# The passages between stages of a two-layer trunk without GpSimd: squares summed on TensorE tile by tile, residual adds and sums on VectorE

## The reference

```python
def rms_norm(x, g, eps=NORM_EPS):
    xf = x.astype(jnp.float32)
    y = xf * lax.rsqrt(jnp.mean(xf * xf, axis=-1, keepdims=True) + eps)
    return (y * g.astype(jnp.float32)).astype(x.dtype)

def sq_relu_mlp(x, w_in, w_out):
    return jnp.square(jax.nn.relu(x @ w_in)) @ w_out

    h = x
    for layer in range(DEPTH):
        hn = rms_norm(h, norm_mix_pre[layer])
        ...  # m = mixer_ab(hn, ...) in layer 0, mixer_ret(hn, ...) in layer 1
        h = h + rms_norm(m, norm_mix_post[layer])
        f = sq_relu_mlp(rms_norm(h, norm_ffn_pre[layer]), ffn_w_in[layer], ffn_w_out[layer])
        h = h + rms_norm(f, norm_ffn_post[layer])
    return h
```

## Time and profile before

| | |
|---|---|
| Median of three runs | 1648.21 us |
| The profiled execution's own time | 1650.05 us |
| Its span, first to last instruction | 1648.2 us |
| Mean granted TensorE clock, as a share of full speed | 0.962 |
| TensorE matmuls busy | 1542.7 us (94%) |
| VectorE busy | 817.7 us (50%) |
| ScalarE busy | 479.5 us (29%) |
| GpSimd busy | 76.0 us (5%) |

### The profile page before, as it was taken

The page is one execution under the profiler, slowest core; times in us unless marked ns, Lnnn a source line. Parts: engine busy times, 40 slices in busy tenths (PEclk is TensorE's granted clock), DMA queues, the critical chain, the costliest instruction groups (busy, mean ns, idle before and its releaser), DMA issues.

```text
span 1648.2 us, 23178 instructions
## 1 busy us (share of the span) xinstructions
PE 1542.7 (94%) x10440; PEld 1247.2 (76%) x10440; DVE 817.7 (50%) x1003; ACT 479.5 (29%) x521; POOL 76.0 (5%) x73
## 2 busy tenths in 40 slices
PE   6898999987689999999899999998997999999996
PEld 5676867766578888888787787877876888888885
DVE  5637547274475444535463444434335754444444
ACT  4325143332332222212332223122123422212220
POOL 1000000000020000000120000000001200000001
PEclk9899998989789999999899999999998999999998
DMA  4111011010032222222221221212211222222221
GB/s 167 52 41 57 15 52 45 28 52 3 26 115 102 101 82 99 102 102 94 72 91 51 78 102 51 102 52 77 102 52 51 94 85 102 103 102 85 94 102 51
DMA packets 19298, 125.16 MB, mean 76 GB/s; under 512 B 2240, under 2 KB 2240, under 8 KB 5120
## 3 DMA queue, kind: packets, MB, share of 16 engines
q1 hardware_dynamic: 18800, 121.29, 21.1%
q0 software_dynamic: 400, 2.39, 0.4%
HBM read 121.58 MB, written 2.10 MB: 75 GB/s over the span
## 4 chain that ended last, share of the span: by engine, by line
PE 87%; DVE 5%; ACT 3%; DMA 2%; issue 2%; POOL 0%; POOLq 0%; SPq 0%; DVEq 0%; ACTq 0%
PE bank L292 23%; PE bank L298 22%; PE bank L295 22%; PE bank L555 7%; PE bank L1119 2%; PE bank L1096 2%; PE bank L1090 2%; PE bank L1093 2%; DMA raw<-weights 1%; PE bank L306 1%; DVE WL L265 1%; PE bank L1111 1%; ACT WH L259 1%; PE bank L569 1%; PE bank L312 1%
## 5 line engine op out<-in xcount | busy, mean ns | idle before, releaser
L292 PE MATMUL bank<-XH,WH 128*128 128x512 f32 x944 | 386.4, 409 | 31.4 <-DVE WL L265 16.2
L295 PE MATMUL bank<-XL,WH 128*128 128x512 f32 x944 | 373.5, 396 | 0.0
L298 PE MATMUL bank<-XH,WL 128*128 128x512 f32 x944 | 373.5, 396 | 0.0
L265 DVE TENSOR_TENSOR WL<-raw,WH 128x2048 fp32r<-128x2048 f32 (+1 forms) x113 | 254.5, 2253 | 203.6 <-ACT WH L259 203.6
L259 ACT ACTIVATE WH<-raw 128x2048 fp32r<-128x2048 f32 (+1 forms) x113 | 212.2, 1878 | 379.0 <-DMA raw<-weights 379.0
L292 PEld LDWEIGHTS bank<-XH,WH 128*128 128x128 f32 x944 | 180.7, 191 | 74.0 <-issue 33.0
L298 PEld LDWEIGHTS bank<-XH,WL 128*128 128x128 f32 x944 | 180.7, 191 | 39.4
L295 PEld LDWEIGHTS bank<-XL,WH 128*128 128x128 f32 x944 | 181.2, 192 | 35.1 <-issue 0.7
L292 PE MATMUL bank<-AH,WH 128*128 128x512 f32 x512 | 199.4, 389 | 0.0
L298 PE MATMUL bank<-AH,WL 128*128 128x512 f32 x512 | 199.2, 389 | 0.0
L295 PE MATMUL bank<-AL,WH 128*128 128x512 f32 x512 | 199.2, 389 | 0.0
(11 more groups left out here) (256 smaller groups left out, 1727.3 us busy)
## 6 DMA issues: line engine op xcount, KB each, us to landing
raw<-weights SPq DMA_DIRECT2D x109, 1024.0 KB, 4.8
h<-x_fm SPq DMA_DIRECT2D x4, 512.0 KB, 6.9
raw<-weights SPq DMA_DIRECT2D x4, 512.0 KB, 3.7
out_fm<-h SPq DMA_DIRECT2D x8, 256.0 KB, 2.0
rc<-ret_const POOLq DMA_DIRECT2D x1, 1536.0 KB, 6.8
stage<-pairs POOLq DMA_DIRECT2D x4, 199.0 KB, 2.7
cst<-const SPq DMA_DIRECT2D x1, 641.0 KB, 10.1
vec<-vectors SPq DMA_DIRECT2D x1, 41.5 KB, 1.7
```

The lines of the kernel that those rows point to most:

```text
L265: nc.vector.tensor_tensor(WL[i][:, :n], raw[i][:, :n], WH[i][:, :n], ALU.subtract).then_inc(S("w_lo"), 1)
L292: mm = pe.matmul(bank[b][:], wh, xh, start=(k == 0), stop=False)
L295: mm = pe.matmul(bank[b][:], wh, xl, start=False, stop=False)
L298: mm = pe.matmul(bank[b][:], wl, xh, start=False, stop=(k == len(xs) - 1))
```

## The change

GpSimd no longer takes part in any norm or residual. Four things change:

1. The squares of f go to TensorE one tile at a time (`post_tile_pe`), eight calls of `token_sums` into bank 4 in place of three. In the feed-forward blocks tile t is taken behind output unit t + 1 of the last quarter, so tiles 0 to 6 stand in the loop and tile 7 behind it. After the mixers and after retention tile t is taken behind unit t + 2, and tiles 6 and 7 behind the loop. `post_sum_pool` and `post_sum_dve` are gone.
2. The squares of h: VectorE adds squares 0 to 5 in five adds (`pre_sum_dve`), interleaved with the residual's tiles from the fourth on; TensorE takes this sum and squares 6 and 7, three calls in place of two. `pre_sums_pool` is gone.
3. All eight adds to h are VectorE's, each behind the XL of the tile before.
4. GpSimd waits for the end of the first residual, issues the DMA of the retention constants, and then does its adds inside the retention stage, as before.

```diff
@@ -313,22 +313,24 @@
             return mm
 
         def pre_sums_pe(pe, m):
-            pe.wait_ge(S("hsq_sum_a"), 3 * m + 3)
+            pe.wait_ge(S("hsq_sum"), 5 * m + 5)
             token_sums(pe, 4, sum_a, True, False)
-            pe.wait_ge(S("hsq_sum_b"), 3 * m + 3)
-            token_sums(pe, 4, sum_b, False, True).then_inc(S("pre_sums"), 1)
+            for kt in (6, 7):
+                pe.wait_ge(S("hsq"), m * KT + kt + 1)
+                mm = token_sums(pe, 4, sq[:, kt, :], False, kt == 7)
+            mm.then_inc(S("pre_sums"), 1)
 
         def pre_spread_pe(pe, m):
             pe.wait_ge(S("pre_rstd"), m + 1)
             spread(pe, 5, pre_rstd).then_inc(S("pre_spread"), 1)
 
-        def post_norm_pe(pe, m):
-            pe.wait_ge(S("fsq_sum_a"), 3 * m + 3)
-            token_sums(pe, 4, sum_a, True, False)
-            pe.wait_ge(S("fsq_sum_b"), 2 * m + 2)
-            token_sums(pe, 4, sum_b, False, False)
-            pe.wait_ge(S("fsq"), m * KT + KT)
-            token_sums(pe, 4, sq[:, KT - 1, :], False, True).then_inc(S("post_sums"), 1)
+        def post_tile_pe(pe, m, kt):
+            pe.wait_ge(S("fsq"), m * KT + kt + 1)
+            mm = token_sums(pe, 4, sq[:, kt, :], kt == 0, kt == KT - 1)
+            if kt == KT - 1:
+                mm.then_inc(S("post_sums"), 1)
+
+        def post_spread_pe(pe, m):
             pe.wait_ge(S("post_rstd"), m + 1)
             spread(pe, 5, post_rstd).then_inc(S("post_spread"), 1)
 
@@ -374,44 +376,19 @@
             nc.vector.scalar_tensor_tensor(XL[:, kt, :], h[:, kt, :], gain(layer, kind, kt), XH[:, kt, :],
                                            ALU.mult, ALU.subtract).then_inc(S("x_lo"), 1)
 
-        def pre_sums_dve(dve, m):
-            for i in range(3):
-                dve.wait_ge(S("hsq"), m * KT + 2 * i + 3)
-                if i:
-                    dve.wait_ge(S("hsq_sum_a"), 3 * m + i)
-                nc.vector.tensor_tensor(sum_a, sum_a if i else sq[:, 0, :], sq[:, 2 * i + 2, :],
-                                        ALU.add).then_inc(S("hsq_sum_a"), 1)
-
-        def pre_sums_pool(pool, m):
-            for i in range(3):
-                pool.wait_ge(S("hsq"), m * KT + 2 * i + 4)
-                if i:
-                    pool.wait_ge(S("hsq_sum_b"), 3 * m + i)
-                nc.gpsimd.tensor_tensor(sum_b, sum_b if i else sq[:, 1, :], sq[:, 2 * i + 3, :],
-                                        ALU.add).then_inc(S("hsq_sum_b"), 1)
+        def pre_sum_dve(dve, m, i):
+            dve.wait_ge(S("hsq"), m * KT + i + 2)
+            if i:
+                dve.wait_ge(S("hsq_sum"), 5 * m + i)
+            nc.vector.tensor_tensor(sum_a, sum_a if i else sq[:, 0, :], sq[:, i + 1, :], ALU.add).then_inc(S("hsq_sum"), 1)
 
         def pre_rstd_dve(dve, m):
             dve.wait_ge(S("pre_root"), m + 1)
             nc.vector.reciprocal(pre_rstd, pre_root).then_inc(S("pre_rstd"), 1)
 
-        def post_sum_pool(pool, m):
-            for i in range(3):
-                pool.wait_ge(S("fsq"), m * KT + 2 * i + 3)
-                if i:
-                    pool.wait_ge(S("fsq_sum_a"), 3 * m + i)
-                nc.gpsimd.tensor_tensor(sum_a, sum_a if i else sq[:, 0, :], sq[:, 2 * i + 2, :],
-                                        ALU.add).then_inc(S("fsq_sum_a"), 1)
-
-        def post_sum_dve(dve, m, i):
-            dve.wait_ge(S("fsq"), m * KT + 2 * i + 4)
-            if i:
-                dve.wait_ge(S("fsq_sum_b"), 2 * m + i)
-            nc.vector.tensor_tensor(sum_b, sum_b if i else sq[:, 1, :], sq[:, 2 * i + 3, :],
-                                    ALU.add).then_inc(S("fsq_sum_b"), 1)
-
-        def add_to_h(ops, kt):
-            ops.tensor_tensor(h[:, kt, :], h[:, kt, :], hn[:, kt % 2, :],
-                              ALU.add).then_inc(S("h_odd" if kt % 2 else "h_even"), 1)
+        def add_to_h(kt):
+            nc.vector.tensor_tensor(h[:, kt, :], h[:, kt, :], hn[:, kt % 2, :],
+                                    ALU.add).then_inc(S("h_odd" if kt % 2 else "h_even"), 1)
 
 
 
@@ -425,16 +402,13 @@
                         h_is_ready(dve, m, kt - 2)
                     nc.vector.scalar_tensor_tensor(hn[:, kt % 2, :], f[:, kt, :], gain(*post, kt),
                                                    bank[5][:], ALU.mult, ALU.mult).then_inc(S("post_term"), 1)
-                    if kt % 2 == 0:
-                        dve.wait_ge(S("post_term"), m * KT + kt + 1)
-                        add_to_h(nc.vector, kt)
                 if kt and pre:
                     x_low(dve, m + 1, *pre, kt - 1)
-
-        def residual_pool(pool, m):
-            for kt in range(1, KT, 2):
-                pool.wait_ge(S("post_term"), m * KT + kt + 1)
-                add_to_h(nc.gpsimd, kt)
+                if kt < KT:
+                    dve.wait_ge(S("post_term"), m * KT + kt + 1)
+                    add_to_h(kt)
+                if pre and kt >= 3 and kt < KT:
+                    pre_sum_dve(dve, m + 1, kt - 3)
 
         def add_to_f(dve, use, b, m, first):
             n = use.next(b)
@@ -472,7 +446,10 @@
                         left = 0 if k else 2 if q == 0 and j == 4 else 1
                         units(pe, use, [(j + k) % 4], [columns(cj, k)], X if j < 8 else A, left,
                               a_tile if j == 8 and k == 0 else None)
-            post_norm_pe(pe, m)
+                        if q == QUARTERS - 1 and j + k > 8:
+                            post_tile_pe(pe, m, j + k - 9)
+            post_tile_pe(pe, m, KT - 1)
+            post_spread_pe(pe, m)
 
         def ffn_act(act, use, c0, m, layer):
             for q in range(QUARTERS):
@@ -512,8 +489,6 @@
                                                 ALU.subtract).then_inc(S("a_lo"), 1)
                     else:
                         add_to_f(dve, use, b, j - 8, q == 0)
-                        if q == QUARTERS - 1 and j in (12, 14):
-                            post_sum_dve(dve, m, j // 2 - 6)
                     if j % 2 == 0 and (q or j):
                         split_lo(dve, c0 + 8 * q + j // 2 + 2)
 
@@ -1027,7 +1002,11 @@
         def last_out_pe(pe, use):
             for m in range(KT):
                 out_unit(pe, use, m, PAIRS - 1)
-            post_norm_pe(pe, 0)
+                if m >= 2:
+                    post_tile_pe(pe, 0, m - 2)
+            for kt in range(KT - 2, KT):
+                post_tile_pe(pe, 0, kt)
+            post_spread_pe(pe, 0)
 
         def last_out_act(act, use):
             for m in range(KT):
@@ -1039,8 +1018,6 @@
         def last_out_dve(dve, use):
             for m in range(KT):
                 add_to_f(dve, use, out_bank(m, PAIRS - 1), m, False)
-                if m in (4, 6):
-                    post_sum_dve(dve, 0, m // 2 - 2)
                 if m == 5:
                     split_lo(dve, FFN0_CHUNK + 1)
 
@@ -1142,7 +1119,11 @@
                     else:
                         for i in range(2):
                             units(pe, use, [RET_OUT[j + i]], [ws[i]], B, 1 if j == 4 and i == 0 else 0)
-            post_norm_pe(pe, m)
+                            if hd == RET_HEADS - 1:
+                                post_tile_pe(pe, m, j + i - 2)
+            for kt in range(KT - 2, KT):
+                post_tile_pe(pe, m, kt)
+            post_spread_pe(pe, m)
 
         def ret_act(act, use, m):
             for hd in range(RET_HEADS):
@@ -1265,8 +1246,6 @@
                     add_to_f(dve, use, RET_OUT[j], j, hd == 0)
                     if j % 4 == 1:
                         split_lo(dve, c + 8 + j // 4)
-                    if hd == RET_HEADS - 1 and j in (4, 6):
-                        post_sum_dve(dve, m, j // 2 - 2)
 
         def ab_uses(use):
             for j in range(2):
@@ -1317,22 +1296,14 @@
                 nc.gpsimd.tensor_copy(pp[:, Q_LNW:], stage[:, Q_LNW:]).then_inc(S("norm_vectors"), 1)
                 pool.wait_ge(S("pp_ready"), p + 1)
                 pool.wait_ge(S("norm_vectors"), p + 1)
-                if p == 0:
-                    pre_sums_pool(pool, 0)
-            for m in range(4):
-                post_sum_pool(pool, m)
-                residual_pool(pool, m)
-                if m < 3:
-                    pre_sums_pool(pool, m + 1)
-                if m == 0:
-                    pool.dma_start(rc[:], ret_const).then_inc(S("rc_loaded"), 16)
-                if m == 1:
-                    for hd in range(RET_HEADS):
-                        pool.wait_ge(S("ysq_ready"), 4 * hd + 2)
-                        nc.gpsimd.tensor_tensor(sum_a, ysq[:, 0, :], ysq[:, 1, :], ALU.add).then_inc(S("ysq_summed"), 1)
-                        pool.wait_ge(S("ysq_ready"), 4 * hd + 3)
-                        pool.wait_ge(S("ysq_summed"), 2 * hd + 1)
-                        nc.gpsimd.tensor_tensor(sum_a, sum_a, ysq[:, 0, :], ALU.add).then_inc(S("ysq_summed"), 1)
+            h_is_ready(pool, 0, KT - 1)
```

(11 more changed lines are left out.)

## The result

The changed kernel takes 1661.42 us (median of four runs, 1655.94 to 1661.97) against 1648.82 for the kernel before: a ratio of 1.0066, 95% interval 1.0039 to 1.0092. It is slower, as forecast. The time lies inside the range of 8 in 10 (1650 to 1662), but only 0.6 us under its upper end, and above the forecast's own range of 1653.5 to 1658.5; the forecast of +8.0 us lies in the lower part of the interval, which is +6.4 to +15.2 us.

The account below looks back on a forecast made before the run. TensorE, busy 1542.7 of 1648.2 us, was taken to bound the kernel, with idle time only between stages. Terms +11.0 - 2.4 - 1.1 - 3.0 + 3.4 + 0.1 = +8.0 gave 1656.2 us; 8-in-10 range 1650 to 1662.

Parts of the forecast that it names:

- the price: One call of token_sums on TensorE costs 0.94 us between full matmuls, with bounds 0.80 and 1.03.
- part 1: Feed-forward blocks: f's squares summed on TensorE tile by tile, net +5.5 us each, +11.0 together.
- Rival D: Sums hidden on TensorE, their weight loads slipping under full matmuls: -6.7 us, 1641.5; chance 0.04.
- parts 2 and 4: f's sums after the mixers, -2.4 us; residual adds all on VectorE, first XL 1.0 sooner at three passages, -3.0.
- part 2: After the mixers: f's sums tile by tile end 2.0 us earlier, spread at high clock gains 0.4; together -2.4.
- rival C: VectorE becomes the bound of the passages, some 2 us at each of three: 1662; chance 0.06.
- rival A: Clock stays high across the passages, first tiles not slow: +1.1 us, 1649.3, or no measurable change; chance 0.11.
- part 3: After retention: f's sums tile by tile, -0.7 us and -0.4 for the spread, -1.1; 0 if the clock falls.
- part 5: Sums of h's squares: TensorE takes three inputs instead of two, +0.85 us at each of four places, +3.4.
- rival B: Sums pull the clock down between the last output units after the mixers: +12 us, 1668; chance 0.05.

Follow-up runs that it names:

- e7: e4 with VectorE summing f's squares 0 to 6 in both feed-forward blocks: 1643.60 us, ratio 0.9964 to the kernel before.
- e2: The changed kernel with f's squares summed by GpSimd and VectorE again; residual adds and h sums stay changed: 1652.55 us, ratio 1.0017 to the kernel before.
- e1: The changed kernel run again, unaltered, in a later batch: 1658.42 us, ratio 1.0056 to the kernel before.
- e6: The kernel before with one added, unread call at each of the four sums of h's squares: 1653.96 us, ratio 1.0037.
- e3: The changed kernel with residual adds and h sums shared with GpSimd again; only f's sums stay changed: 1655.88 us, ratio 1.0037 to the kernel before.
- e4: The changed kernel with a sixth VectorE add of h's squares, so TensorE takes two inputs: 1651.71 us, ratio 1.0009 to the kernel before.
- e8: e7 with VectorE also summing f's squares after mixers (0 to 4) and retention (0 to 6), weight splits behind f's last tile: 1634.91 us, ratio 0.9916.
- e10: e8 with VectorE's weight splits put back at their old places, behind f's tile 5: 1642.14 us, ratio 0.9959 to the kernel before.
- e5: The changed kernel with the three calls for h's squares parted by a tile at the three passages: 1655.37 us, ratio 1.0037 to the kernel before.

## Why the prediction was right, and where it was not

**Right: what an instruction on TensorE costs (the price, part 1).** 0.94 a call was expected, 0.95 stands in the stream. The blocks grew by 5.61 and 5.70 where 5.64 was summed. Taking the calls out again (e7) gave back 5.55 and 5.63. Rival D (hidden calls) is out.

**Right: the ends (parts 2 and 4).** The mixers' end with its calls: -3.7 measured, -3.4 expected. The XL beside GpSimd: 1.0 at each passage, which e2 shows alone. The end of layer 0's block came 1.5 shorter and not 1.0: its spread ran at the high clock (0.65) where it had been at the low one before (1.11), a gain that part 2 of the prediction has at the mixers' end and no part has here. VectorE's loop never held up TensorE behind the first tile; rival C is out. So is rival A: the first tiles ran at the low clock in every profile, for 3.4 to 5.9 us.

**Mis-sized: part 3.** Retention's five calls added 3.7, not 4.7, since before TensorE had waited 0.8 us for one of f's tiles there (the bank was not free yet), and with the calls between the units it does not: they covered that wait. Its spread still ran at the low clock (1.11), so those 0.4 did not come; in e1 it ran at the high one, and that end is 0.6 shorter. Net -2.5 with the first XL, where -2.1 was summed.

**The step that failed: part 5, "+0.85 at each of four places, all in an unbroken stream at full clock".** At the three passages it cost 2.6, 2.6 and 2.1 us, not 0.85: 7.2 in place of 2.6. The stream was at full clock up to the calls, and fell to 1.2 GHz behind them (twice in their last part, at the third passage of e2 and of e6). The count over the profiles of all kernels, at the three passages: three calls in one piece, a fall at 12 of 12 places (after, e1, e2, e6); two calls, at 1 of 18 (before, e3, e4, e7, e8, e10); three calls parted by a tile, at none of 3; one call, at none of 3. e6 shows it in the kernel before by a call that does nothing else, e4 and e5 undo it in two different ways. But three calls in one piece are not the whole condition: at the start of the kernel they stand in the same form, and there the clock fell in e2 and e5 and stayed high in after, e1 and e6, 2 of 5; behind two calls there it fell in none of 6. What decides between the two is not shown by these runs. The argument for the full clock had been and the window from 896 to 900, and both show two calls: the step was taken from two to three without a row.

**The rule.** The page "TensorE: Matmul & The Clock Gate" of the Trainium skill, in "Why this matters for your kernels", says that the clock swings in loops of thin matmuls that wait for a transfer at each step. The prediction left out the wait, gave this 0.05 and looked for it after the mixers, where calls and full matmuls alternate. There nothing fell: the runs of matmuls between the calls at 434.18 and 445.58 have the steps of the high clock. So the trace does not bear out rival B. The fall behind three calls is not the page's case either: it follows one piece and no loop, and TensorE waited for nothing there.

**Why the sum still came out near.** With 4.7 more in part 5 the terms give 12.7, and the places of the profile add up to 11.7. The medians say +12.6 in the first batch, the ratio of the second says +9.2. The forecast of 8.0 is 1.2 to 4.6 short. By the places of the trace what it lacks, 3.7, is this step, less 1.0 that the other terms had too high. That the timed difference of the second batch comes within 1.2 us of a sum that lacks 4.7 in one term is luck, and so is the 0.6 us by which the first batch stays inside the range. The intervals of the two batches overlap, so which of the two is nearer the truth is not known.

## What to carry to other kernels

On an engine that never waits, a "free" reduction costs its full time: add the partial sums on an engine that has slack, and give the busy one only the last tile. When small matmul work is added to a busy engine, look at the granted clock behind it too; parting three calls by a tile took the low stretch away at three places here, though the timed gain is not certain. Before moving sums onto VectorE, look what else is written ahead of them there: at the two ends after the mixers and after retention, moving the sums alone changed nothing that could be measured (e7 and e10), and moving one weight split behind the last tile at each was worth some 7 us (e10 and e8).

## What the runs showed that was not expected

- The low clock behind three calls in one piece (2.59 us of one-column matmuls), 3.4 us long at eleven of the twelve places at the passages and 6.8 at one, at a cost of some 1.5 us each; its absence in three of five profiles where the same calls stand at the start; and its absence when one tile of full matmuls stands between the calls.
- The scatter of one unchanged kernel of 1.6 ms: 24 runs from 1644.3 to 1653.2 us. It goes with the mean granted clock of the run: the fastest had 0.965, the two slowest 0.959 and 0.961. Unchanged stages of the profiles differ by up to 6 us (the mixers, 405.9 to 412.0 in the six kernels that have no calls between their last units) and retention's heads take one of two periods, near 109 or near 110 us, with TensorE's wait for the BL tile at 0.8 to 1.0 us in some and 2.0 in others. A change of a few microseconds has to be read from its own place in the trace, and then timed over many runs.
